# Seven block products in place of eight for the gate, up and conv-in products of a two-layer streaming encoder

## The reference, cut to what matters

```python
def rmsnorm(x, g):
    y = xf * lax.rsqrt(jnp.mean(xf * xf, axis=-1, keepdims=True) + EPS)
    return y * g
def swiglu(x, w_gate, w_up, w_down):
    return (jax.nn.silu(x @ w_gate) * (x @ w_up)) @ w_down
def conv_mixer(x, w_in, w_dw, w_out):
    b, c, h = jnp.split(x @ w_in, 3, axis=-1)
    return (b * depthwise_causal(c * h, w_dw)) @ w_out
for l in range(2):              # D_MODEL 1024, D_FF 2816, 512 + 64 tokens
    x = x + 0.5 * swiglu(rmsnorm(x, ffn1_norm[l]), ...)
    x = x + (conv_mixer if l == 0 else attn_mixer)(rmsnorm(x, mix_norm[l]), ...)
    x = x + 0.5 * swiglu(rmsnorm(x, ffn2_norm[l]), ...)
y = rmsnorm(x, final_norm)
```

## Time and profile before

| | |
|---|---|
| times of three runs | 2297.95, 2298.23, 2296.41 us; median 2297.95 us |
| the profiled execution | span 2295.8 us from first to last instruction; its own time isn't given apart from the span |
| TensorE matmul / weight load busy | 2267.1 us (99%) / 2201.1 us (96%), 16584 of each |
| VectorE (DVE) busy | 978.2 us (43%) |
| ScalarE (ACT) busy | 646.0 us (28%) |
| GpSimd (POOL) busy | 101.6 us (4%) |
| DMA | 187.91 MB, mean 82 GB/s |

### The profile page before, as it was taken

One profiled execution on the slowest core, in us unless ns is written; L12 is line 12 of the kernel. 1 busy time (PEld: TensorE's weight loads), 2 busy tenths in 40 slices (PEclk: granted clock), 3 DMA queues, 4 the chain that ended last, 5 costly groups with the idle time before them and its releaser, 6 DMA issues.

```text
span 2295.8 us, 39703 instructions
## 1 busy us (share of the span) xinstructions
PE 2267.1 (99%) x16584; PEld 2201.1 (96%) x16584; DVE 978.2 (43%) x1309; ACT 646.0 (28%) x967; POOL 101.6 (4%) x109
## 2 busy tenths in 40 slices
PE   7999999999999999999999999999999999999997
PEld 7999999999999999999999999987878899999997
DVE  5433333555443333345333433455455444333334
ACT  4212212422332122124221212334343432122122
POOL 1000000200100000002000000100000110000002
PEclk9999999999999999999999999999999999999999
DMA  4222222222222222223222222222222122222222
GB/s 148 83 83 83 83 83 74 86 89 83 83 77 87 80 82 82 82 72 93 83 83 83 83 83 81 85 75 73 73 72 74 57 83 80 85 78 87 76 81 69
DMA packets 55407, 187.91 MB, mean 82 GB/s; under 512 B 6864, under 2 KB 7168, under 8 KB 55312
## 3 DMA queue, kind: packets, MB, share of 16 engines
q1 hardware_dynamic: 49248, 173.76, 25.2%
q10 hardware_dynamic: 3888, 7.70, 0.9%
q0 software_dynamic: 2176, 5.09, 0.9%
HBM read 179.42 MB, written 7.09 MB: 81 GB/s over the span
## 4 chain that ended last, share of the span: by engine, by line
PE 98%; DVE 1%; DMA 1%; ACT 0%; ACTq 0%; DVEq 0%; issue 0%
PE ps L829 92%; PE ps L909 2%; PE ps L891 2%; PE ps L877 1%; DMA x<-x_t 1%; PE ps L912 0%; PE ps L844 0%; DVE sumsq L664 0%; DVE x L810 0%; PE ps L894 0%; PE ps L896 0%; DVE rstd L611 0%; PE ps L866 0%; PE ps L914 0%; ACTq L460 0%; DVE w_lo L601 0%
## 5 line engine op out<-in xcount | busy, mean ns | idle before, releaser
L829 PE MATMUL ps<-xg_hi,w_hi 128*128 128x288 f32 x3584 | 780.0, 299 | 11.1 <-DVE w_lo L601 8.6
L829 PE MATMUL ps<-xg_hi,w_lo 128*128 128x288 f32 x3584 | 768.2, 296 | 0.0
L829 PE MATMUL ps<-xg_lo,w_hi 128*128 128x288 f32 x3584 | 767.2, 296 | 0.0
L829 PEld LDWEIGHTS ps<-xg_hi,w_hi 128*128 128x128 f32 x3584 | 576.0, 189 | 42.7 <-issue 26.5
L829 PEld LDWEIGHTS ps<-xg_lo,w_hi 128*128 128x128 f32 x3584 | 577.8, 189 | 0.0
L829 PEld LDWEIGHTS ps<-xg_hi,w_lo 128*128 128x128 f32 x3584 | 577.6, 189 | 0.0
L399 ACT ACTIVATE w_hi<-w_raw 128x1024 fp32r<-128x1024 f32 (+1 forms) x336 | 346.0, 1030 | 433.6 <-PE ps L829 398.9
L601 DVE TENSOR_TENSOR w_lo<-w_raw,w_hi 128x1024 fp32r<-128x1024 f32 (+1 forms) x336 | 402.5, 1198 | 27.2 <-ACT w_hi L399 27.1
L675 DVE TENSOR_TENSOR scaled<-ps,rstd 128x576 f32<-128x576 f32 x176 | 133.3, 758 | 640.6 <-PE ps L829 640.4
L829 PE MATMUL ps<-hid_hi,w_hi 128*128 128x288 f32 x1664 | 358.2, 297 | 1.7 <-DVE hid_lo L646 1.7
L829 PE MATMUL ps<-hid_hi,w_lo 128*128 128x288 f32 x1664 | 357.2, 296 | 0.0
(11 more groups left out here) (85 smaller groups left out, 852.3 us busy)
## 6 DMA issues: line engine op xcount, KB each, us to landing
w_raw<-w SPq DMA_DIRECT2D x304, 512.0 KB, 3.6
w_raw<-w SPq DMA_DIRECT2D x32, 384.0 KB, 3.0
x<-x_t ACTq DMA_DIRECT2D x8, 288.0 KB, 10.4
k_t<-k_sb ACTq DMA_DIRECT2D x8, 288.0 KB, 2.1
v_t<-v_sb ACTq DMA_DIRECT2D x8, 288.0 KB, 2.4
bias<-bias_ext POOLq DMA_DIRECT2D x16, 128.0 KB, 3.1
bias<-bias_ext POOLq DMA_DIRECT2D x16, 112.0 KB, 2.7
y_t<-x SPq DMA_DIRECT2D x6, 288.0 KB, 2.3
```

What stands on the lines that cost most here:

```text
L829: mm = pe.matmul(ps[:, 2 * out_slot + b, 0:HALF], wt[:, w_slot, w], xt[:, k, b * HALF:(b + 1) * HALF], start=(k == 0 and n == 0), stop=(k ...
```

## The change

Gate and up (and conv-in) weight tiles are taken in pairs. A pair, two output tiles by 8 input blocks, is a 2 x 2 matrix of *pieces* A11, A12, A21, A22 (each 128 outputs by 4 input blocks); the normalised activations are a 2 x 2 matrix B11, B12, B21, B22 (4 input blocks by one token half each). The 2 x 2 product is made from seven products of sums of pieces, P1 to P7, in place of eight. P1 = A11 B11 and P2 = A12 B21 give the first output for the first token half; the other three quarters come from U2 = P1 + P6, from which U3 and U4 follow. A *run* is one such product: 4 blocks by 3 passes = 12 matmuls, all into one bank. A *group* is the seven runs of a pair. FFNs have 4 x 22 = 88 groups, conv-in 12 (the last 4 of them take two tiles of b each).

- Sums of weights: `add_weights` on VectorE makes S1 to S4 from the raw pieces, 3 instructions per group. Weights are loaded by piece (256 KB) into 14 staging units; two pieces make a *batch* (1024 columns), which is split into `w_hi` and `w_lo` as before (L550, L867), four batches ahead. A group has 3.5 batches (before: 2).
- Sums of activations: x is normalised ahead of the product (`normalise`, 16 instructions of 288 columns per norm), with four differences (`difference`, 1152 columns) and seven operand parts each on ScalarE (`operand_hi`) and VectorE (`operand_lo`). So the product waits for the norm.
- To cover that, the phase before a norm (`last`) ends with tiles 5, 6 and 7 in token halves, first half first; the phase behind it begins with P1 and P2 of all its groups (`early`), which need the first token half alone, and then runs P6, P7, P5, P3 and P4 (`late`). Chunks 2 and 3 (`next`) run whole groups.
- Between runs ScalarE copies from PSUM: P1 into a second bank (`seed`), U2, U4, and silu of the two gate halves. VectorE takes the two up halves (`take_c21`, `take_c22`).
- The sum of squares moves from GpSimd to VectorE, by halves. qkv keeps its 24 tiles of 48 matmuls, of which the first three run by halves; its activations are also normalised ahead.
- No loops are left: all phases are written out.

The core of the diff:

```diff
...
+COMBOS = ("B11", "B21", "T1", "B22", "T3", "T2", "T4")
+A11, S3, A22, A21, S2, A12, S4 = range(7)
+S1 = A21
+PIECE_OF = {"P1": A11, "P2": A12, "P3": S4, "P4": A22, "P5": S1, "P6": S2, "P7": S3}
+SUM_STEP = {S3: 1, S1: 1, S2: 2, S4: 3}
...
+    def product(self, p, kind, j, part):
+        self.start_run(p, kind, j)
+        base = 7 * part
+        if kind == ("P1" if p.kind == "next" or j >= DT else "P6"):
+            for piece, row, second in ((A11, 2 * j, 0), (A22, 2 * j + 1, 1), (A21, 2 * j + 1, 0), (A12, 2 * j, 1)):
+                self.load_piece(base + piece, p.row + row, second)
+        if kind == "P6":
+            need = [16 * self.loaded[base + u] for u in (A11, A22, A21, A12)]
+            at = len(self.batches) - 1
+            assert all(self.split_by[base + u] <= at + 1 for u in (S3, S2, S4))
+            self.sums_after.setdefault(at, []).append((self.sets, base, need))
+            for u, step in ((A11, 1), (A21, 1), (A22, 2), (A12, 3)):
+                self.summed_by[base + u] = 3 * self.sets + step
+            p.piece["set", j] = self.sets
+            self.sets += 1
+        piece = PIECE_OF[kind]
+        sums = 3 * p.piece["set", j] + SUM_STEP[piece] if piece in SUM_STEP else 0
+        self.add_piece(p, kind, j, base + piece, sums)
+
...
+def early_order(n):
+    order = [("P1", 0), ("P1", 1), ("P1", 2)]
+    for j in range(3, n):
+        order += [("P2", j - 3), ("P1", j)]
+    return order + [("P2", j) for j in range(n - 3, n)]
+
+
+def late_order(n, close):
+    order = [("P6", 0), ("P7", 0), ("P5", 0), ("P3", 0)]
+    for j in range(1, n):
+        order += [("P6", j), ("P4", j - 1), ("P5", j), ("P7", j), ("P3", j)]
+    return order + [("P4", n - 1)] * close
+
+
+def next_order(first, end, open_group):
+    order = []
+    for j in range(first, end):
+        order.append(("P1", j))
+        if j > first or open_group is not None:
+            order.append(("P4", j - 1))
+        order += [("P6", j), ("P2", j), ("P5", j), ("P7", j), ("P3", j)]
+    return order + [("P4", end - 1)]
+
...
+            def early(p):
+                n = p.norm
+                gate = ACT.Silu if p.kind == "first" else ACT.Copy
+                for e, (kind, j) in enumerate(early_order(p.n)):
+                    act.wait_ge(run_done, p.run[kind, j] + 1)
+                    if kind == "P1":
+                        act.activation(est[:, j, HALF:TOK], ps[:, EARLY_BANKS[j % 4], 0:HALF],
+                                       ACT.Copy).then_inc(p1_done, 1)
+                    else:
+                        act.activation(est[:, j, 0:HALF], ps[:, EARLY_BANKS[j % 4], 0:HALF],
+                                       gate).then_inc(c11_done, 1)
+                    if e == SUM_AFTER:
+                        split_hi(p.run[kind, j])
+                        root(n, 1)
+                        if p.kind == "first":
+                            act.preload_act_table(ACT.Silu)
+                        continue
+                    split_hi(p.run[kind, j])
+                    if e == 6:
+                        operand_hi(n, 2, 1)
+                        operand_hi(n, 3, 16)
+                    if e == 7:
+                        operand_hi(n, 4, 2)
+                    if e == 9:
+                        operand_hi(n, 5, 3)
+                    if e == 10:
+                        operand_hi(n, 6, 4)
+                    if kind == "P2" and j in (p.n - 3, p.n - 2):
+                        s = j - (p.n - 3)
+                        act.wait_ge(c11_done, p.c11s + s + 5)
...
+            def groups(p):
+                for j in range(p.n):
+                    act.wait_ge(run_done, p.run["P1", j] + 1)
+                    if j < 2:
+                        act.wait_ge(xadd_done, p.xadds - 1)
+                    else:
+                        act.wait_ge(c12_done, p.c11s + j - 1)
+                    seed(p, j, ps[:, j % 2, 0:HALF])
+                    split_hi(p.run["P1", j])
+                    if j:
+                        split_hi(p.run["P4", j - 1])
+                    take_u2(p, j)
+                    split_hi(p.run["P6", j])
+                    if j:
+                        hidden_hi(p, j - 1, up[:, (j - 1) % 2, :])
+                    act.wait_ge(run_done, p.run["P2", j] + 1)
+                    act.activation(est[:, j, 0:HALF], ps[:, j % 2, 0:HALF], ACT.Silu).then_inc(c11_done, 1)
+                    split_hi(p.run["P2", j])
+                    take_u4(p, j)
+                    split_hi(p.run["P5", j])
+                    split_hi(p.run["P7", j])
+                    act.wait_ge(run_done, p.run["P3", j] + 1)
+                    act.activation(est[:, j, HALF:TOK], ps[:, 2 + j % 2, 0:HALF], ACT.Silu).then_inc(c12_done, 1)
+                    split_hi(p.run["P3", j])
+                split_hi(p.run["P4", p.n - 1])
+                hidden_hi(p, p.n - 1, up[:, (p.n - 1) % 2, :])
+
+            def down(p):
+                for m in range(DT):
+                    split_hi(p.run["m", m])
+
...
+            def add_weights(s, base, need):
+                for u, count in zip((A11, A22, A21), need):
+                    dve.wait_ge(raw_loaded[base + u], count)
+                two = stage[:, base + A21:base + A21 + 1, :].broadcast_to([P, 2, PIECE])
+                dve.tensor_tensor(stage[:, base + S3:base + S1 + 1:S1 - S3, :], two,
+                                  stage[:, base + A11:base + A22 + 1:A22 - A11, :], ALU.add).then_inc(sum_done, 1)
+                dve.wait_ge(sum_done, 3 * s + 1)
+                dve.tensor_tensor(stage[:, base + S2, :], stage[:, base + S3, :], stage[:, base + A22, :],
+                                  ALU.add).then_inc(sum_done, 1)
+                dve.wait_ge(sum_done, 3 * s + 2)
+                dve.wait_ge(raw_loaded[base + A12], need[3])
+                dve.tensor_tensor(stage[:, base + S4, :], stage[:, base + S2, :], stage[:, base + A12, :],
+                                  ALU.add).then_inc(sum_done, 1)
...
+            def normalise(n, h, ms):
+                for m in ms:
+                    dve.scalar_tensor_tensor((xn1, xn2)[h][:, m, :], x[:, m, cols(h)], gain[:, n, m:m + 1],
+                                             rstd[:, cols(h)], ALU.mult, ALU.mult).then_inc(xn_done, 1)
...
+            def difference(n, i):
+
+                b11, b21 = flat(xn1[:, 0:KQ, :]), flat(xn1[:, KQ:DT, :])
+                b12, b22 = flat(xn2[:, 0:KQ, :]), flat(xn2[:, KQ:DT, :])
+                done = 4 * (n - (n > 4))
+                if i == 0:
+                    dve.wait_ge(xn_done, 16 * n + 12)
+                    dve.tensor_tensor(b11, b11, b12, ALU.subtract).then_inc(diff_done, 1)
...
+                for e, (kind, j) in enumerate(early_order(p.n)):
+                    split_lo(p.run[kind, j])
+                    if e == 3:
+                        invert(n, 1)
+                        normalise(n, 1, range(0, 4))
+                    if e == 4:
+                        difference(n, 0)
+                        normalise(n, 1, (4, 5))
+                    if e == 5:
+                        normalise(n, 1, (6, 7))
+                    if e == 6:
+                        difference(n, 1)
+                        operand_lo(n, 2)
+                    if e == 7:
+                        operand_lo(n, 3)
+                        difference(n, 2)
+                    if e == 8:
+                        operand_lo(n, 4)
+                    if e == 9:
+                        difference(n, 3)
+                    if e == 10:
+                        operand_lo(n, 5)
+                    if e == 11:
+                        operand_lo(n, 6)
+
+            def late(p):
+                if p.kind == "conv":
...
+            def last(p):
+                n = p.feeds
+                final = n == N_NORM - 1
+                share = 0.5 if p.source == "ffn" else 1.0
+                both = slice(0, TOK)
+                for m in range(SPLIT_TILE):
+                    add_tile(p, m, share)
+                    split_lo(p.run["m", m])
+                    if m > 1:
+                        add_square(n, m - 2, both)
+                s = SPLIT_TILE - 2
+                for i, m in enumerate(range(SPLIT_TILE, DT)):
+                    add_half(p, 0, m, share)
+                    add_square(n, s + i, cols(0) if i else both)
+                add_square(n, s + 3, cols(0))
+                add_half(p, 1, SPLIT_TILE, share)
+                invert(n, 0)
+                if final:
+                    make_y(0)
                 else:
-                    split_hi(ahead(p, At(p.g + 3 * t.of() + r), 3 * t.of() + r))
-                if r == 2:
-
-                    act.wait_ge(tile_read, at.of(1, W_SLOTS + 1))
-                    odd = t.first % 2 if not isinstance(t.i, int) else t.of() % 2
-                    for src, dst in ((k_sb, k_t), (v_sb, v_t)):
-                        act.dma_start(dst[bass.ds(t.of(), 1)].rearrange("a p n -> p (a n)"), src[:, odd, :]
```

(69 more changed lines are left out.)

1587 lines of the change are left out of this document (958 added, 629 removed).

## The result

The changed kernel takes 2321.7 us (median of 4 runs, 2318.4 to 2322.1) beside 2297.3 us before (4 runs, 2296.4 to 2298.2): 1.0103 times as long, 95% interval 1.0091 to 1.0116. The forecast was 2260; it came out slower by 1.0%, and the time lies outside the range. The profiled execution spans 2316.3 us where it spanned 2295.8, 20.5 us more.

What follows compares the result with a forecast made beforehand. TensorE's matmuls, 133.3 ns each, were taken to bound the kernel. -160.0 + 7 + 9 + 57 + 31 + 5 + 10 + 3 - 4.3 + 4 = -38.3 us gave 2260 us, range (8 in 10) 2203 to 2292.

Steps and rivals of the forecast that it cites:

- Removed: FFNs and conv-in: 100 pairs of tiles take 84 matmuls in place of 96, 1200 fewer at 133.3 ns, -160.0 us.
- whole groups: `next` phases: P3 waits 0.25 us for the U4 copy in every second group, 28 groups, +7 us.
- U4 chain: Rival, `next` phases: VectorE enters groups with 2 us of backlog, P3 waits 2.25 us, +63 us, 2316; chance 0.10.
- one-bank matmuls: Rival, product runs: 12 matmuls in a row into one bank are slower, +67 us, 2327; chance 0.03.
- Norm seam: Ahead of norms 1, 2, 3, 5: TensorE waits 3.05 or 1.45 us for the lower operand part, +9.0 us together.
- Early: P1 and P2 behind five norms: operands and evictions delay P2(7) to 36.3 us from 24.6 in FFNs; +57 us together.
- Late: P6 to P4 of first chunks and conv-in: VectorE's backlog, work and waits for weight loads cost +31 us together.
- Clock: Half clock after long stops: hidden by VectorE and ScalarE in the early phases, +4 us at the other seams.
- qkv: qkv phase: seam 3.05 us, block 4 of its first tile 2.5, second half's operands 1.8 and 2.7; +10 us.
- Down tiles: 6-block down tiles: they need the last hidden tile after 4.0 us, it takes 4.3 plus VectorE's queue; +3 us.
- Tail: From the last product to the end: 12.7 us by halves in place of 17.0, -4.3 us.
- The rival with an end on the slow side: `next` phases: VectorE backlog of 2 us makes P3 wait for U4 in every second group, 2316 us; chance 0.10.

Runs made afterwards that it cites:

- load_order: Changed kernel with the load of piece A21 asked for ahead of that of A22: 2291.2 us, 0.9978 of the kernel before.
- thin_sums: Changed kernel with one column of each weight sum in place of 512, results wrong: 2256.5 us, 0.9815 of the kernel before.
- load_root_thin: load_order plus second-half root and reciprocal done earlier, and one column of each weight sum in place of 512, results wrong: 2222.9 us, 0.9673 of before.
- load_all: load_order plus earlier second-half root and reciprocal, late U4 copies ahead of ScalarE's split, weight sums after C21 read and gate product: 2288.6 us, 0.9962 of before.
- fill_stops: Changed kernel plus 358 matmuls whose result nobody reads, where TensorE stops in first chunks and conv-in: 2320.6 us, 1.0097 of before.
- load_root_fill: load_order plus earlier second-half root and reciprocal, and 315 unread matmuls at stops of first chunks and conv-in: 2275.9 us, 0.9909 of before.

## Why the prediction was wrong

- **Removed, and whole groups: right.** 8400 matmuls, 133 ns apart in the `next` phases, 10 us over in eight phases (forecast 7). The rivals of the U4 chain and of one-bank matmuls are out.
- **Norm seam: right.** TensorE waited 3.04, 1.45, 3.04 and 1.44 us for the first lower operand part, 9.0 in sum.
- **Early: near.** The evictions (`est`) end its stops, as forecast. P2(7) started 39.4, 37.1, 36.8 and 36.8 us behind P1(0) in the first chunks (forecast 36.3) and 36.8 in conv-in: 7 us more over the five.
- **Late: the step that failed.** "VectorE waits about 1 us in some: 1.5 us" a phase. It waited 6.6 to 10.7 us in each late part, 42.2 in all. I had taken the time to land (it measured 3.2 us for 256 KB) and never asked what a load stood behind in its queue. From P2(7) on the first chunks took 81.8 us on average against the 70.0 forecast, conv-in 128.6 against 124.3: 52 us. With the early part's 7 that is the 59 between the 91 forecast (88 and a sum of 0.6 in each) and the 149.8 found. load_order shows it: the swap of two loads takes 26 of the 59 (30.5 us of the program's time). Of the rest it is shown that the sums' own time on VectorE is in it (thin_sums, load_root_thin), and that their place ahead of the read of C21 isn't what matters (load_all); which waits carry it stays open. It isn't that VectorE had too much work: in the late parts of the first chunks it was busy for 60.4 us of the 81.8, where TensorE's own work makes 65.6. I had set the totals of a group side by side, 7.9 us against 8.0, and priced few of the waits of one engine for another.
- **Clock: right about the path, far off in size.** I wrote that VectorE and ScalarE hide it in the early phases. 46 us of half clock, 41 more than before, against a term of 4. At the stops that were filled nearly none of it costs anything (fill_stops, load_root_fill: 18 and 12 us of it taken away for 1 and 4 us); that of the qkv seam wasn't tested.
- **The rest.** First product at 21.9 us (forecast 19). qkv: stops of 8.0 us and 3.5 of slow matmuls (forecast 10). Down tiles: no stop for the last hidden tile (forecast 3). Tail: the last product ends near 2301.9, 14.4 us before the end (before 17.0, forecast 12.7). Unrolling: nothing shows; the `next` phases stop for 0.5 us in 90.9.
- **The rival with an end on the slow side** was the wrong one: I had priced a backlog of VectorE in the second chunks, where it never arose, and not in the late part, where I had found 7.9 us of work for 8.0 of time and should have put the chance. That its 2316 lies near the 2321.7 measured is luck.
- **Slips in the working.** 257 matmuls at 133.3 ns are 34.3 us of the first 50, so 15.7 us were lost there and not 15.3; halfway between no gain (2298) and 2280 is 2289 and not 2292. Neither changes the outcome.

## What to carry to other kernels

Where an engine's work nearly fills a stretch (here 7.9 us of 8.0 by the forecast's own sum), there is no room for any wait of that engine: price the waits of its inputs there first, from the order in which the loads are asked for and what each stands behind, not from the time they take to land. A trade of TensorE's work for VectorE's pays only in stretches where VectorE has slack in order, not just in sum; here it paid in eight phases (89.6 us of matmuls saved, 10 lost) and cost more than twice what it saved in the other five (70.4 saved, 149.8 lost). Before you blame the clock, fill the stops and see if the time moves.

## What the runs showed of the hardware

- A stop of 4.09 us is followed by 25 matmuls at half clock (some 6 us), while the stops of 1.4 us at P2(0) and of 2.31 us at P4(4) in FFN 3 had none behind them. Behind a stop of 3.03 us in FFN 3 came 12 matmuls 133 ns apart and then 14 at 240 ns. In the kernel before, 14 such matmuls came behind a stop of 1.75 us. So the length of a stop alone doesn't tell whether the clock falls.
- GpSimd's additions: 2.51 us for 1024 columns and 1.33 to 1.51 for 512 on average, twice VectorE's 1.22 and 0.69, and a product on VectorE beside them takes up to 2.60 us in place of 0.76. The other way round too: the second addition of a set took 1.28 us in 50 of 100 sets and 1.68 in 45, and in 40 of those 45 an operation of VectorE with two inputs in SBUF had begun before it.
